# Scores of the second block as three products of rounded hi and lo parts, in place of one full fp32 product

## The reference, cut to what matters

```
q, k, v = jnp.split(h @ w_in, 3, axis=-1)
# layer 0 (diff_attention)
s = jnp.einsum('mbhqd,mbhkd->mbhqk', qb, kf) * scale
s = jnp.where(dist >= 0, s + bias, NEG_INF)
p = jax.nn.softmax(s, axis=-1)
a = p[0] - lam * p[1]
# layer 1 (moba_attention; T = one block of 256 keys)
sc_own = jnp.einsum('bhqd,bhkd->bhqk', qc, k_own) * scale - slopes[:, None, None] * d_own
p = jax.nn.softmax(sc, axis=-1)
```

## Time and profile before

| | |
|---|---|
| median of 3 runs | 1005.75 us (1005.74 to 1005.75) |
| the profiled execution, its own time | 1008.36 us |
| its span | 1006.4 us |
| TensorE busy | 996.4 us, 99% of the span |
| VectorE busy | 719.6 us, 72% |
| ScalarE busy | 600.0 us, 60% |
| mean DMA rate | 195 GB/s |
| granted clock over the span | 0.994 |
| layer 0, from the first chunk of q, k, v to the last head | about 408 to 507 us |
| layer 1, the same | about 705 to 803 us |

### The profile page before, as it was taken

The page is one execution under the profiler, slowest core; times in us unless marked ns, Lnnn a source line. Parts: engine busy times, 40 slices in busy tenths (PEclk is TensorE's granted clock), DMA queues, the critical chain, the costliest instruction groups (busy, mean ns, idle before and its releaser), DMA issues.

```text
span 1006.4 us, 16631 instructions
## 1 busy us (share of the span) xinstructions
PE 996.4 (99%) x6640; PEld 894.9 (89%) x6640; DVE 719.6 (72%) x1224; ACT 600.0 (60%) x1011; POOL 0.4 (0%) x5
## 2 busy tenths in 40 slices
PE   8999999999999999999999999999999999999997
PEld 7899999998888888999999888888999899888886
DVE  4898888878888888887658665655766558565552
ACT  4678665647665656867647545554666546555453
POOL 0000000000000000000000000000000000000000
PEclk8999999999999999999999999999999999999999
DMA  9965668545556664563325556555553337555521
GB/s 365 366 241 204 243 230 299 197 164 192 201 197 247 214 246 168 210 209 127 126 88 220 201 203 204 172 181 202 217 189 134 126 105 252 199 178 177 203 81 42
DMA packets 28443, 196.72 MB, mean 195 GB/s; under 512 B 3152, under 2 KB 3664, under 8 KB 5584
## 3 DMA queue, kind: packets, MB, share of 16 engines
q1 hardware_dynamic: 28080, 195.14, 54.4%
q10 hardware_dynamic: 288, 0.52, 0.1%
HBM read 194.61 MB, written 1.05 MB: 194 GB/s over the span
## 4 chain that ended last, share of the span: by engine, by line
PE 96%; DVE 1%; ACT 1%; DMA 1%; issue 0%; ACTq 0%; SPq 0%
PE PS L1217 17%; PE PS L1220 9%; PE PS L1035 8%; PE PS L1308 8%; PE PS L1309 8%; PE PS L1310 8%; PE PS L1036 7%; PE PS L1037 7%; PE PS L1187 4%; PE PS L1190 3%; PE PS L1188 3%; PE PS L1250 2%; PE PS L1251 2%; PE PS L1252 2%; PE PS L1407 2%; PE PS L1396 1%
## 5 line engine op out<-in xcount | busy, mean ns | idle before, releaser
L1873 DVE TENSOR_TENSOR wlo<-raw,whi 128x1024 fp32r<-128x1024 f32 x306 | 358.3, 1216 | 60.4 <-ACT whi L1470 57.7
L1470 ACT ACTIVATE whi<-raw 128x1024 fp32r<-128x1024 f32 x300 | 297.9, 1047 | 59.3 <-PE PS L1310 53.5
L1217 PE MATMUL PS<-HX,whi 128*128 128x512 f32 x736 | 261.3, 398 | 0.0
L1220 PE MATMUL PS<-HX,wlo 128*128 128x256 f32 x736 | 206.6, 281 | 0.0
L1217 PEld LDWEIGHTS PS<-HX,whi 128*128 128x128 f32 x736 | 138.3, 188 | 33.9
L1035 PE MATMUL PS<-HX,whi 128*128 128x256 f32 x496 | 145.8, 294 | 0.0
L1036 PE MATMUL PS<-HX,whi 128*128 128x256 f32 x496 | 140.8, 284 | 0.0
L1037 PE MATMUL PS<-HX,wlo 128*128 128x256 f32 x496 | 140.7, 284 | 0.0
L1220 PEld LDWEIGHTS PS<-HX,wlo 128*128 128x128 f32 x736 | 139.0, 189 | 1.2
L1308 PE MATMUL PS<-whi,Oh 128*128 128x512 f32 x344 | 134.8, 392 | 0.0
L1309 PE MATMUL PS<-wlo,Oh 128*128 128x512 f32 x344 | 134.2, 390 | 0.0
(11 more groups left out here) (269 smaller groups left out, 1649.6 us busy)
## 6 DMA issues: line engine op xcount, KB each, us to landing
raw<-wall SPq DMA_DIRECT2D x151, 1024.0 KB, 5.0
raw<-wada SPq DMA_DIRECT2D x18, 1024.0 KB, 5.0
raw<-wall SPq DMA_DIRECT2D x8, 512.0 KB, 15.4
GA<-wada SPq DMA_DIRECT2D x2, 1024.0 KB, 18.8
GA<-alibi SPq DMA_DIRECT2D x1, 2048.0 KB, 9.4
raw<-wall SPq DMA_DIRECT2D x2, 768.0 KB, 5.3
X<-xt SPq DMA_DIRECT2D x1, 1024.0 KB, 6.4
KM<-wada SPq DMA_DIRECT2D x1, 1024.0 KB, 13.7
```

The source lines that it names most:

```text
L1217: e.matmul(PS[:, b, :], whi[place(n)][:, at:at + 128], HX[:, k, :, :].rearrange("p h t -> p (h t)"), start=k == 0, stop=k == 7, skip_group ...
L1220: m = e.matmul(PS[:, b, 0:T], wlo[place(n)][:, at:at + 128], Hh[:, k, :], start=False, stop=k == 7, skip_group_check=True)
L1470: e.activation(whi[place(n)][:, c], raw[i % RAW][:, c], ACT.Copy).then_inc(*up("a_whi", (n, half)))
L1873: e.tensor_tensor(wlo[place(n)][:, c], raw[i % RAW][:, c], f32(whi[place(n)][:, c]), ALU.subtract).then_inc(*up("v_wlo", (n, half)))
```

## The change

In both layers of the second block each evacuated tile of Q or K is split. A new step `qk_low` follows each `ev_qk`: ScalarE copies two tiles (128 x 512) of `QM` or `KM` to an fp32r tile `HI`, and VectorE subtracts, writing an fp32r `QL` or `KL`. For the first three tiles the order is `ev_qk` Q0, K0, Q1, then `qk_low` Q0, K0, Q1, then the refill; for the other five `qk_low` comes right after `ev_qk` and ahead of `scale` and `refill`. The mark that the scores wait for (`v_qk`) is now given by the subtraction; the PSUM bank and the norm's row are released by the first mark, "scaled".

The score step of these heads issues three products, hi by hi, hi by lo and lo by hi, each for the two blocks of queries and the two slots: 12 fp32r matmuls with 64 rows where 4 float32 matmuls stood. It waits for both banks ahead of the first. The first block's scores stay as they were.

`QL` and `KL` lie where `QM` and `KM` lie (so the subtraction writes in place), and the two halves of `HI` where `ACC` and the four tables lie; ScalarE's copy has waits for their last readers (the turned outputs, or the scores of earlier heads).

```diff
+        def ev_qk(n, b, which, j):
+            emit("ev_qk", n, b, layer, which, j)
+            emit("qk_low", layer, which, j)
...
                     emit("ev_qk", n, b, layer, "Q", 1)
+                    for which, j in (("Q", 0), ("K", 0), ("Q", 1)):
+                        emit("qk_low", layer, which, j)
                     refill(waiting[1][0])
...
-                rows(key, a, evac=lambda n, b, pr, c=c: emit("ev_qk", n, b, layer, "Q", c))
+                rows(key, a, evac=lambda n, b, pr, c=c: ev_qk(n, b, "Q", c))
...
-                rows(key, a, evac=lambda n, b, pr, c=c: emit("ev_qk", n, b, layer, "K", c - 4))
+                rows(key, a, evac=lambda n, b, pr, c=c: ev_qk(n, b, "K", c - 4))
...
-        QF, KF = (first.enter_context(nc.sbuf_tensor(name, [128, 8, T], F32)) for name in ("QF", "KF"))
+        QM, KM, QF, KF = (
+            first.enter_context(nc.sbuf_tensor(name, [128, 8, T], F32)) for name in ("QM", "KM", "QF", "KF"))
+        ACC = first.enter_context(nc.sbuf_tensor("ACC", [128, 1024], F32))
+        TB = first.enter_context(nc.sbuf_tensor("TB", [128, 4, T], F32))
+    COS, SIN, TRI, LV = (TB[:, i, :] for i in range(4))
+    QL = sb("QL", [128, 8, T], F32R)
+    KL = sb("KL", [128, 8, T], F32R)
     whi.append(sb("whi3", [128, CH], F32R))
     wlo.append(sb("wlo3", [128, CH], F32R))
+    HI = (sb("HI0", [128, 4, T], F32R), sb("HI1", [128, 4, T], F32R))
...
+    def hi_tiles(which, j):
+        at = 2 * (which == "K")
+        return HI[j % 2][:, at:at + 2, :]
+
+    def lo_tiles(which, j):
+
+        return (QL if which == "Q" else KL)[:, 2 * j:2 * j + 2, :]
...
             elif step == "ev_qk":
-                free[a[1]] = ("v_qk", tuple(a[2:]))
+                free[a[1]] = ("v_qk", (*a[2:], "scaled"))
...
+                if kind in ("diff", "moba"):
+
+                    layer = int(kind == "moba")
+                    on.wait_ge("v_qk", (layer, "Q", i // 2))
+                    on.wait_ge("v_qk", (layer, "K", i // 2))
+                    qs, ks = ([parts(w, i // 2)[:, i % 2, :] for parts in (hi_tiles, lo_tiles)] for w in "QK")
+                    for slot in slots(head):
+                        bank(4 + slot % 2)
+                    for part, (q, k) in enumerate(((qs[0], ks[0]), (qs[0], ks[1]), (qs[1], ks[0]))):
+                        for t, c, keys in ((0, 0, 128), (1, 128, 256)):
+                            for j, slot in enumerate(slots(head)):
+                                p = slice(64 * j, 64 * j + 64)
+                                m = e.matmul(
+                                    PS[:, 4 + slot % 2, c:c + keys], q[p, 128 * t:128 * t + 128], k[p, 0:keys],
+                                    start=part == 0 and t == 0, stop=part == 2, skip_group_check=True)
+                                if part == 2 and t == 1:
+                                    m.then_inc(*up("t_s", (head, slot)))
+                                    free[4 + slot % 2] = ("v_s", (head, slot))
+                    continue
...
+            elif step == "qk_low":
+                layer, which, j = a
+                on.wait_ge("v_qk", (layer, which, j, "scaled"))
+                if j >= 2:
+                    on.wait_ge("t_s", ((("diff", "moba")[layer], 2 * j - 3), 3))
+                elif j == 0:
+                    on.wait_ge("t_turned", (("down", "ff20")[layer], 3))
+                elif layer == 0:
+                    on.wait_ge("v_s", (("mla", 3), 3))
+                    on.wait_ge("v_lam", "dots")
+                if layer and j < 2:
+                    on.wait_ge("t_s", (("diff", 5 + 2 * j), 3))
+                src = (QM if which == "Q" else KM)[:, 2 * j:2 * j + 2, :]
+                e.activation(hi_tiles(which, j), src, ACT.Copy).then_inc(*up("a_qk", (layer, which, j)))
...
+            elif step == "qk_low":
+                layer, which, j = a
+                on.wait_ge("a_qk", (layer, which, j))
+                e.tensor_tensor(
+                    lo_tiles(which, j), (QM if which == "Q" else KM)[:, 2 * j:2 * j + 2, :], f32(hi_tiles(which, j)),
+                    ALU.subtract).then_inc(*up("v_qk", (layer, which, j)))
```

More of the change, by code:

```diff
@@ L820, in _build @@
     Ol = sb("Ol", [128, 8, T], F32R)
-    QM = sb("QM", [128, 8, T])
-    KM = sb("KM", [128, 8, T])
     with ExitStack() as first:
-        QF, KF = (first.enter_context(nc.sbuf_tensor(name, [128, 8, T], F32)) for name in ("QF", "KF"))
+        QM, KM, QF, KF = (
[5 more added lines that the diff above has]
+    KL = sb("KL", [128, 8, T], F32R)
     whi.append(sb("whi3", [128, CH], F32R))
     wlo.append(sb("wlo3", [128, CH], F32R))
+    HI = (sb("HI0", [128, 4, T], F32R), sb("HI1", [128, 4, T], F32R))
     V = sb("V", [128, 2, 1024])
     GA = sb("GA", [128, 16, T])
-    ACC = sb("ACC", [128, 1024])
     SQ = sb("SQ", [128, 4, T])
-    COS = sb("COS", [128, T])
-    SIN = sb("SIN", [128, T])
     PB = sb("PB", [128, 4, 384])
@@ L837, in _build @@
     RB = sb("RB", [128, 2, T])
-    TRI = sb("TRI", [128, T])
     ONES = sb("ONES", [128, 128])
@@ L850, in _build @@
     SW = sb("SW", [128, 1])
-    LV = sb("LV", [128, 256])
     PS = ctx.enter_context(nc.psum_tensor("PS", [128, 8, 512], F32))
@@ L1382, in tensor @@
                         on.wait_ge("v_f" if i // 2 else "a_f", ("queries", 4 * (i // 2)))
-                    elif kind == "mla":
+                    else:
                         h = 2 * i + j
@@ L1389, in tensor @@
                         on.wait_ge("a_ev", (NUMBER[("ukv", 0)], 1))
[L1390 to L1393, removed]
                     bank(b)
@@ L1723, in scalar @@
             elif step == "ev_qk":
-                rb_free[0] = ("v_qk", tuple(a[2:]))
+                rb_free[0] = ("v_qk", (*a[2:], "scaled"))
+            elif step == "qk_low":
[12 more added lines that the diff above has]
+                e.activation(hi_tiles(which, j), src, ACT.Copy).then_inc(*up("a_qk", (layer, which, j)))
             elif step == "ev_v":
@@ L2241, in vector @@
                     (QM if which == "Q" else KM)[:, 2 * j:2 * j + 2, :], two(b),
-                    RB[:, 0, :].unsqueeze(1).to_broadcast([128, 2, T]), ALU.mult).then_inc(*up("v_qk", (layer, which, j)))
+                    RB[:, 0, :].unsqueeze(1).to_broadcast([128, 2, T]), ALU.mult).then_inc(
+                    *up("v_qk", (layer, which, j, "scaled")))
+            elif step == "qk_low":
[4 more added lines that the diff above has]
+                    ALU.subtract).then_inc(*up("v_qk", (layer, which, j)))
             elif step in ("ev_out", "ev_down"):
```

## The result

| | before | after |
|---|---|---|
| median of 4 runs | 1005.75 us | 1017.14 us |
| lowest to highest | 1004.66 to 1005.75 | 1016.42 to 1017.97 |
| profiled execution, own time | 1008.36 us | 1017.1 us |
| its span | 1006.4 us | 1015.1 us |

The changed kernel is slower by 11.4 us: ratio 1.0117, 95% interval 1.0105 to 1.013. The forecast was 1014.2 us, the range 1010 to 1020.

The account below looks back on a forecast made before the run. TensorE, busy for 99% of the span, was taken as the bound, so whatever makes it wait adds time. Waits of 7.8 us plus products of 0.6 made 8.4 us, giving 1014.2 us, range 1010 to 1020.

Parts of the forecast that it names:

- head 0 of layer 0: First turn of layer 0: three subtractions and K1's copy and subtraction delay scale; TensorE idle, +2.93 us.
- head 0 of layer 1: First turn of layer 1: same steps and same +2.97 us on the scaled tile, more margin; +2.02 us.
- head 3 (after K2): Layer 0 after K2: the copy pushes the square root's table load back, root +1.74 us, scale behind it; turn +0.6 us.
- head 6 (after K3): Layer 0 after K3: table load behind the copy delays root, weights, minimum and exponentials; turn of head 6 +1.25 us.
- head 2: Turn of head 2, layer 0: tile 1.40 us later against 1.01 of margin, +0.4 us.
- head 5: Turn of head 5, layer 0: 1.14 us later against 0.63 of margin, +0.5 us.
- head 3 of layer 1: Turn of head 3 in layer 1, by the same count as the smaller waits: +0.1 us.
- The products: Score steps on TensorE: 0.90 us each with fp32r, 0.04 more than now, x16 steps, +0.6 us.
- the rival of 128 columns at float32's pace (1.20): Score step: 128 column fp32r matmuls run at float32's pace, 5.4 us in place of 0.6, 1019.0 us; chance 0.18.
- the streaming (0.72): Score step: weight loads hidden, 128 column matmuls take 0.06 us, 2.3 us given back, 1011.3 with the waits; chance 0.10.
- the lost overlap (1.62): Score step: the two slots run one after the other, 12.2 us in place of 0.6, 1025.8 us; chance 0.05.
- the clock: Rival: idle at each layer's first turn lowers TensorE's clock, 1.7 us each, 1015.9 or 1017.6; chance of any 0.22.

Follow-up runs that it names:

- split alone: The changed kernel with its split kept, but the scores as float32 products again, read from the lo parts alone: 1015.81 us, ratio 1.0105.
- products alone: The changed kernel without the split: evacuation writes one fp32r tile that all three products read, lo parts left out: 1005.59 us, ratio 1.0003.
- the one with the catching up at the end: Repaired order with weights made one chunk late, but in layer 0 the lag kept to the end of the twelve chunks: 1008.13 us, ratio 1.0035.
- the one kept busy: The changed kernel plus 12 and 8 extra matmuls that nothing reads, on TensorE ahead of each layer's first turn: 1013.76 us, ratio 1.0085.
- the start alone: The changed kernel with only Q1's split moved behind K1's and the weights of Q1's chunk made one chunk later: 1013.22 us, ratio 1.0079.

## Why the prediction was right

**The waits.** Each turn was forecast by the same count, instructions set ahead of `scale` less the margin of before. Forecast and measured, start to start less what the step takes undisturbed: head 0 of layer 0, 2.93 and 2.85; head 0 of layer 1, 2.02 and 1.95; head 3 (after K2), 0.6 and 0.75; head 6 (after K3), 1.25 and 1.25; head 2, 0.4 and 0.38; head 5, 0.5 and 0.47; head 3 of layer 1, 0.1 and 0.13. The sum was to be 7.8 and is 7.8. Each link of the chain of head 0 can be found in the timelines above: the three subtractions ahead of the `wlo`, the copy behind the exponentials, VectorE idle for it. The split alone gave the loss, the products alone did not, and moving the split behind `scale` took away the waits that it was said to make.

**The products.** 0.90 was forecast for a step, 0.89 measured; +0.4 us in place of +0.6. The reason given, that the weight load and not the streaming sets the pace, fits what was tried: 64 columns take what 128 do, and the loads start evenly, some 0.11 us apart. Only the even 0.12 for each matmul was too simple: they come in pairs of 0.23. With it the rival of 128 columns at float32's pace (1.20) falls, and so do those of the streaming (0.72) and of the lost overlap (1.62). The Trainium skill's rule of passes (FP8 and Floating Point Precision, TensorE Precision Notes) would give a shorter step; the page states the four passes, and one pass for a reduced read is the prediction's reading of it. The trace does not bear that out: 0.89 us against 0.86, longer.

**The step that was mis-sized: the clock.** It had stood among the rivals, with 0.22 for one drop or more, and not in the sum. Both drops came, one behind each of the two longest waits, and took 1.5 us each where 1.7 was reckoned. With them the forecast of 1014.2 would have been the 1017.6 given there; 1017.14 was measured. The slower start of a turn that has waited, 0.6 us in all, was in no term either, and the products were put 0.2 too high. So the waits were right by their mechanism and one by one, and the total stayed 2.9 us too low, inside the range because the range allowed for the clock. Rows 2 showed 3.4 us at 0.50 behind a stretch of nearly empty matmuls, and two idle times of 2.9 and 2.0 us were themselves part of the forecast; to give the likeliest case no drop at all was the error. Of the eight changed kernels whose profile has an unfilled idle time of 1.4 us or more, six have at least one drop behind it; the two without are the one with the catching up at the end (1.95 us) and the one kept busy (1.46 us at `turn` 6, which wasn't filled).

**The margins of the repairs.** The forecast for the split behind `scale` held. Those for all the later orders missed, by 2.6 us and more, and mostly for one reason: they counted the path to the turns that had waited and took everything else for covered. In three of the five a drop of the clock came on top, behind the wait that was not foreseen or, in the start alone, behind one that was. A refill moved later frees the turn, and stands in front of a minimum, which stands in front of an evacuation. The rival in those expectations, that the added work must show somewhere, fits layer 0: in each of five orders (all but the start alone, which left the later waits as they were) a wait of 1.4 to 2.2 us stood in it, in four different places: the first `turn`, the `values` of head 0, `turn` 6 and, twice, the output product. That there is no order without one isn't shown; six were tried.

## What to carry to other kernels

Where one engine is busy for 99% of the span, a stage's room on the others is not their idle share but the margin between each result and the instruction that wants it: list those margins, then count every instruction that is put ahead of the producer in its own queue, and on the other engine whose result it now awaits. Put a split, a copy or a refill behind the work that the bounding engine waits for, then look again at what it now stands in front of, since moving it gave back 9 of 11.4 us here and never the rest. And where a forecast contains idle times of 1.5 us or more in dense matmul work, price a clock drop behind each beside them.

## What the runs showed of the hardware

**The clock after a short wait.** Idle times of 1.5 to 2.7 us of TensorE between dense matmuls were followed by 3.4 us at a granted clock of 0.50 in some places and not in others: behind 1.79 us in layer 1 of the change, but not behind 1.82 us in the split alone; behind 1.49 us at `turn` 6 there, but not behind 1.47 us in the change. The length of the wait alone doesn't decide; what does isn't settled by these runs. In the profiles of before, of the products alone and of several others there are also drops with no part in the change, at 11, near 55 or past 1000 us. With those at 11 and 55 us the profile of before is 3.9 us later, by the time layer 0 begins its heads, than that of the split behind `scale`, which has neither and the same work up to there. So a difference of this size between two spans has to be looked for in the place where it arose.

**Few columns don't make an fp32r matmul shorter.** Steps with 64 and with 128 columns in half their matmuls took 0.883 and 0.886 us.

**Two slots on different rows of the array overlap, but not at any distance in the queue.** With six fp32r matmuls a slot, alternated, a step takes 0.89 us, and slot by slot 1.22. With four instructions a slot (float32), slot by slot, they overlap in full: 0.86.

**A table load can hide or not.** In the kernel before ScalarE loads the root's table (1.28 us) at 457.07, behind the exponentials and ahead of need. In the change the copy stands between, waits for VectorE, and the load comes behind it, into the path: VectorE is idle for 0.88 us before 462.49, and was for 0.40 at the same place in the kernel before.
